# A two-layer decoder trunk: shorter filler at four waits, operands taken in smaller pieces, the S5 output product reordered, one sum of squares and one weight split moved

## The reference, cut to what matters

```
h = x
hn = rmsnorm(h);  h += retention(hn)        # 4 heads, q/k/v/g projections, per-head norm, output product
hn = rmsnorm(h);  h += swiglu(hn)           # dense, 1024 -> 3584 -> 1024
hn = rmsnorm(h);  h += s5(hn)               # u = hn @ w_in; complex diagonal scan over time;
                                            # y = Re(C state) + D u; gelu; z = y @ w_out; za * sigmoid(zb)
hn = rmsnorm(h);  h += moe(hn)              # logits = hn @ router; top 2 of 8 experts; each a swiglu
out = rmsnorm(h)
```

## Time and profile before

| | us |
|---|---|
| median of 3 runs | 1593.15 (1592.84 to 1593.97) |
| the profiled execution | 1591.9 |
| its span | 1589.7 |
| PE busy in the span | 1569.7 |
| DVE busy | 1212.1 |
| ACT busy | 984.6 |
| POOL busy | 264.4 |

### The profile page before, as it was taken

How to read it: one execution, slowest core, us unless ns; L and a number is a source line. 1 busy time by engine, 2 the same in 40 slices (tenths; PEclk the granted TensorE clock), 3 DMA queues, 4 the chain that set the end, 5 groups by cost and what they waited for, 6 DMA issues and landing times.

```text
span 1589.7 us, 23667 instructions
## 1 busy us (share of the span) xinstructions
PE 1569.7 (99%) x9522; PEld 1310.1 (82%) x9522; DVE 1212.1 (76%) x811; ACT 984.6 (62%) x731; POOL 264.4 (17%) x244
## 2 busy tenths in 40 slices
PE   8999999999999999999999999999999999999997
PEld 7888889999988778888888888888888888888886
DVE  5556566655557758888888888888888888888897
ACT  6444445333454356777777777777777777777775
POOL 5599215300036107100000000000000000000100
PEclk9999999999999999999999999999999999999999
DMA  9544648865511286999999999999999999999993
GB/s 350 165 157 158 211 139 283 281 201 186 186 54 56 78 309 242 395 385 363 386 354 366 395 366 352 388 360 368 382 379 347 389 376 344 393 372 349 399 393 150
DMA packets 202144, 469.19 MB, mean 295 GB/s; under 512 B 7785, under 2 KB 20289, under 8 KB 202065
## 3 DMA queue, kind: packets, MB, share of 16 engines
q1 hardware_dynamic: 199872, 461.13, 80.0%
q0 software_dynamic: 2048, 6.88, 1.5%
q10 hardware_dynamic: 144, 0.07, 0.0%
HBM read 461.23 MB, written 15.21 MB: 300 GB/s over the span
## 4 chain that ended last, share of the span: by engine, by line
PE 66%; DVE 1%; ACT 1%; issue 1%; POOL 0%; ACTq 0%; POOLq 0%; DVEq 0%
PE PS L1713 63%; PE PS L1832 2%; PE PS L2171 0%; ACT c_padded L878 0%; ACT weights_hi L878 0%; PE PS L2014 0%; POOL states L798 0%; DVE scan L1254 0%; DVE states L1254 0%; DVE weights_lo L1254 0%; PE PS L2129 0%; DVE scan_tmp L1254 0%; DVE residual L1254 0%; DVE normed_rows L1706 0%; DVE scan L1480 0%
## 5 line engine op out<-in xcount | busy, mean ns | idle before, releaser
L1254 DVE TENSOR_TENSOR weights_lo<-weights_raw,weights_hi 128x2048 fp32r<-128x2048 f32 (+1 forms) x419 | 964.3, 2310 | 263.7 <-ACT weights_hi L878 261.8
L878 ACT ACTIVATE weights_hi<-weights_raw 128x2048 fp32r<-128x2048 f32 (+1 forms) x419 | 800.7, 1912 | 366.4 <-PE PS L1713 354.0
L1713 PE MATMUL PS<-weights_hi,gathered_hi 128*128 128x512 f32 x896 | 355.3, 397 | 0.3 <-DVE gathered_lo L1594 0.3
L1713 PE MATMUL PS<-weights_hi,gathered_lo 128*128 128x512 f32 x896 | 355.0, 396 | 0.0
L1713 PE MATMUL PS<-weights_lo,gathered_hi 128*128 128x512 f32 x896 | 352.3, 393 | 0.0
L1713 PE MATMUL PS<-weights_hi,act_transposed_hi 128*128 128x512 f32 x624 | 252.9, 405 | 0.5 <-DVE act_transposed_lo L1402 0.5
L1713 PE MATMUL PS<-weights_hi,act_transposed_lo 128*128 128x512 f32 x624 | 247.0, 396 | 0.0
L1713 PE MATMUL PS<-weights_lo,act_transposed_hi 128*128 128x512 f32 x624 | 245.7, 394 | 0.0
L1713 PEld LDWEIGHTS PS<-weights_hi,gathered_lo 128*128 128x128 f32 x896 | 168.2, 188 | 41.3
L1713 PEld LDWEIGHTS PS<-weights_lo,gathered_hi 128*128 128x128 f32 x896 | 168.2, 188 | 41.1
L1713 PEld LDWEIGHTS PS<-weights_hi,gathered_hi 128*128 128x128 f32 x896 | 168.2, 188 | 39.9 <-DVE gathered_lo L1594 0.3
(11 more groups left out here) (279 smaller groups left out, 1273.6 us busy)
## 6 DMA issues: line engine op xcount, KB each, us to landing
weights_raw<-in_moe_w_up SPq DMA_DIRECT2D x111, 1024.0 KB, 7.3
weights_raw<-in_moe_w_down SPq DMA_DIRECT2D x111, 1024.0 KB, 7.0
weights_raw<-in_moe_w_gate SPq DMA_DIRECT2D x110, 1024.0 KB, 7.3
weights_raw<-in_ret_w_in SPq DMA_DIRECT2D x24, 1024.0 KB, 6.7
weights_raw<-in_ffn_w_gate SPq DMA_DIRECT2D x14, 1024.0 KB, 5.1
weights_raw<-in_ffn_w_up SPq DMA_DIRECT2D x14, 1024.0 KB, 5.1
weights_raw<-in_ffn_w_down SPq DMA_DIRECT2D x14, 1024.0 KB, 5.0
weights_raw<-in_ret_w_out SPq DMA_DIRECT2D x8, 1024.0 KB, 4.9
```

The lines of the kernel that those rows point to most:

```text
L878: return nc.scalar.activation(o, i, ACT.Copy)
L1254: return nc.vector.tensor_tensor(o, a, b, op)
L1713: return nc.tensor.matmul(o, l, r, start=start, stop=stop)
```

## The change

It does seven things:

1. `x_ready` asks for one pair instead of two before the first matmul, for the first (retention) and third (S5) norm; for the dense stage it still asks for two.
2. `yt_lo` is counted twice per head, behind tiles 0 and 1 and behind tiles 2 and 3; each half of the output product waits for its own half. The wait for `yt_hi` and the three fillers behind it go.
3. 16 fillers ahead of the dense stage become 9.
4. The six fillers in quarter 0 of S5 become three.
5. `s5_out` runs the direct products of both tiles first, with no wait for states, then all with the real states, then all with the imaginary ones, each behind its own wait.
6. The sum of squares of token tile 1 ahead of the routing goes from ACT (L1157) to DVE, and the low part of the second expert unit goes from ahead of the gate product to behind `pick`.
7. Five fillers between the two tiles of the logits become two.

```diff
@@ scalar, routing
             copy(hn_t[:, 0, :, :], PS[:, 0:2, :].rearrange("p a (b c) -> p (a b) c", c=P)).then_inc(hnt_copied[0], 1)
-            act.wait_ge(resid_ready, 3)
-            nc.scalar.activation(hn[:, 1, :], resid[:, 1, :], ACT.Square, accum_out=ssq[:, 1:2]).then_inc(ssq1_done, 1)
             act.wait_ge(ssq0_done, 4)
             act.wait_ge(ssq1_done, 4)
@@ vector, evac_yt
-                ins.then_inc(yt_lo, 1)
+                    if ft % 2:
+                        ins.then_inc(yt_lo, 1)
@@ vector, end of S5 and routing
-            for i in range(2):
-                split_lo(MOE_U0 + i)
+            split_lo(MOE_U0)
             dve.wait_ge(glu_read, 1)
             dve.wait_ge(glu_sig, 2)
...
+            dve.wait_ge(resid_ready, 3)
+            nc.vector.scalar_tensor_tensor(out=hn[:, 1, :], in0=resid[:, 1, :], scalar=1.0, in1=resid[:, 1, :],
+                                           op0=ALU.mult, op1=ALU.mult, accum_out=ssq[:, 1:2]).then_inc(ssq1_done, 1)
             dve.wait_ge(hnt_done, 2)
...
             ins.then_inc(pick_ready, 1)
 
+            split_lo(MOE_U0 + 1)
             dve.wait_ge(moe_landed, 32)
@@ tensor, x_ready
-                    pe.wait_ge(xlo_ready, KT // 2 * i + max(2, kt // 2 + 1))
+                    pe.wait_ge(xlo_ready, KT // 2 * i + max(2 if i == 1 else 1, kt // 2 + 1))
@@ tensor, retention
             def head_out(h, half, n):
+                pe.wait_ge(yt_lo, 2 * h + half + 1)
                 if half == 0:
-                    pe.wait_ge(yt_lo, h + 1)
                     pe.wait_ge(par_ready, 1)
...
             turn_y(HEADS - 1)
             idle_work(10, 0)
-            pe.wait_ge(yt_hi, HEADS)
-            idle_work(3, 0)
             head_out(HEADS - 1, 0, RET_UNITS - 2)
+            pe.wait_ge(yt_lo, 2 * HEADS)
             closing_unit(RET_UNITS - 1, ht_hi[0], ht_lo[0])
             plain(1)
-            idle_work(16, 4)
+            idle_work(9, 4)
             dense()
@@ tensor, s5_out
-                pe.wait_ge(st_re_ready, q + 1)
-                if q == QUARTERS - 1:
-                    pe.wait_ge(last_im_ready, 1)
-                else:
-                    pe.wait_ge(st_im_ready, q + 1)
                 y = PS[:, 5, :].rearrange("p (a c l) -> p a l c", a=QKT, l=STEP)
...
-                    for l in range(STEP):
-                        for j in range(2):
+                for j in range(2):
+                    if j == 0:
+                        pe.wait_ge(st_re_ready, q + 1)
+                    elif q == QUARTERS - 1:
+                        pe.wait_ge(last_im_ready, 1)
+                    else:
+                        pe.wait_ge(st_im_ready, q + 1)
+                    for a in range(QKT):
+                        for l in range(STEP):
                             for s in range(4):
@@ tensor, quarter 0
-                    idle_work(6, 5)
+                    idle_work(3, 5)
@@ tensor, logits
-                    idle_work(5, 4)
+                    idle_work(2, 4)
```

More of the change, by code:

```diff
@@ L1969, in _ @@
                 if h:
-                    pe.wait_ge(yt_lo, h)
+                    pe.wait_ge(yt_lo, 2 * h)
                 for half in range(2):
```

## The result

The changed kernel takes 1582.97 us (median of 6 runs, 1582.56 to 1583.54) against 1592.76 (1591.63 to 1593.97): 9.8 us less, ratio 0.994 with a 95% interval of 0.9929 to 0.995. 1587.3 had been forecast, in a range of 1585.0 to 1590.4, on a kernel before of 1593.15 (three runs; 1592.76 is the median of six). The profiled executions took 1582.77 us (span 1580.8) and 1591.9 (span 1589.7), 9.1 apart.

What follows compares the result with a forecast made beforehand. PE was taken as the bound, busy 1569.7 of 1589.7 us. Seven terms summed to 5.83, say 5.9 us, taken from 1593.15 to give 1587.3, in a range of 1585.0 to 1590.4.

Steps and rivals of the forecast that it cites:

- The fourth unit's low part: Kernel start: this work, ready at 31.16, does not move and lets PE in at 31.27, limiting the gain to 0.62.
- End of retention: Last head's output product: PE starts behind the second DVE instruction, at 207.76 instead of 208.54, gaining 0.78 us.
- Dense: Ahead of the dense stage: nine fillers instead of 16 gain 1.12 us, with DVE's two pairs then the limit.
- S5's first unit: One pair starts PE about 0.55 earlier, but the norm's diagonal does not move, so 0.35 us is gained.
- Quarter 0's filler: S5, six fillers to three: 0.7 us saved, but PE then idles 0.65 for POOL's padded B; gain 0.05.
- Routing and logits: Transposes 1.2 us earlier, logits 0.66, moved split 0.1 late behind `pick`: gain 1.76 us.
- The clock rival: Clock falls to 1.2 GHz behind the four filler cuts, costing 1.7 us each, up to 1594.2; chance 0.07.
- The rule weighed there: Routing: GpSimd shares SBUF interfaces with VectorE, so POOL's row numbers come some 2 us later beside the split; sum stays.
- s5_out, direct products first: S5 output products: same number of matmuls, waits of 0.2 (quarter 0) and 0.95 (last quarter) go; gain 1.15 us.
- The clock dip goes away: Rival, S5 near 496.70 to 500.15: the half clock also vanishes, 1.1 us more, 7.0 in all, 1586.1; chance 0.15.
- another hole of 0.65 us appears nearby: Argument against the clock dip going away: a new PE hole at 485.3.
- The start, 0.62: First unit, one pair instead of two: PE starts 0.78 us earlier, of which 0.62 lasts past the fourth unit.

Runs made afterwards that it cites:

- s5_out_only: Kernel before with only the new s5_out (direct products first, then each states part behind its own wait): 1589.58 us, ratio 0.9985.
- s5_order_only: Kernel before with s5_out's matmuls in the new order, but both waits for the states still ahead of all of them: 1591.9 us, ratio 0.9997.
- after_old_out: Changed kernel with only S5's output product as it was, both waits ahead and direct and state matmuls in turn: 1585.52 us, ratio 0.9952.
- before_again: Kernel before, unchanged, profiled a second time: 1592.53 us, ratio 1.0003.
- pairs_only: Kernel before with only the low parts of x asked for pair by pair, one pair ahead instead of two at first use: 1591.35 us, ratio 0.9996.
- before_start_fewer: Kernel before with ten filler matmuls fewer in its first 7 us, nothing else changed: 1591.18 us, ratio 0.9993.
- six_fillers: Changed kernel with six fillers ahead of s5_in(0) as before, instead of three: 1584.04 us, ratio 0.9947.
- fillers_but_q0: Kernel before with the filler cuts ahead of the dense layer, in the last head and in the router, but quarter 0's six kept: 1588.85 us, ratio 0.9976.
- q0_three_only: Kernel before with only the six fillers ahead of s5_in(0) cut to three: 1591.31 us, ratio 0.9992.
- six_fillers_load_late: Changed kernel with six fillers ahead of s5_in(0) and the 1 MB load issued only after the first quarter's output product: 1583.04 us, ratio 0.9939.
- late_load_split_behind: Changed kernel with the third S5 unit's low part behind quarter 0's states and the 1 MB load after that quarter's output product: 1583.93 us, ratio 0.9945.
- loads_late: Kernel before with a 1 MB weight load and POOL's 0.5 MB gain row load waiting for S5 output products, PE instructions unchanged: 1590.46 us, ratio 0.9989.
- after_start_more: Changed kernel with ten narrow matmuls (32 columns) more in its first 7 us: 1587.95 us (1585.49 to 1591.71), ratio 0.9973.
- split_behind_states: Changed kernel with the third S5 unit's low part moved on DVE from ahead of quarter 0's states to behind them: 1582.99 us, ratio 0.9941.

## Why the prediction was wrong

**What held.** The fourth unit's low part does bound the start; it came 0.5 later in this execution (29.09 for 28.58), and let PE on at 31.72 where 31.27 was said (31.89 before). End of retention: 0.78 said, 0.79 seen, with 0.34 idle. Dense: 1.12 and 1.14, bounded by DVE's second pair as said. S5's first unit: 0.35 and 0.3. Quarter 0's filler: nothing, and the new wait on POOL's b_padded of 0.69 where 0.65 was said. Routing and logits: 1.76 said; 1.2 + 0.70 - 0.05 = 1.85 seen. The experts kept everything. The clock rival did not come: 1.00 behind all four cuts. The rule weighed there came as said too: POOL's first routing instruction took 2.15 beside the moved split, where it had taken 1.14, and PE lost nothing by it.

**What failed.** *"s5_out, direct products first"*: the step reads "The number of matmuls is the same: 48 and 128", and took equal numbers for equal time, with 0.45 of room for a loss and 0.15 for a gain. The term was 1.15 and measures 0.22 + 0.95 + 4 x 0.25 = 2.17. Its two waits went as said; the regrouping gives 1.0 more, since it saves eight changes of tile form. That is shown in quarters 1 to 3 of s5_out_only and s5_order_only and in all four of after_old_out. The traces show it first: 32*32 products and 128*32 products in turn cost 0.12 to 0.14 us a change. The Trainium skill (TensorEngine Tiling (Array Packing), section "Tiling Modes", key properties) has the rule that I did not weigh: changing the tiling mode, not just the tile, drains TensorE. These runs agree with it; the page gives no price.

**The rival I gave 0.15 came half true.** "The clock dip goes away" was right on the size in quarter 0 (1.1) and wrong on the object. Without a half clock (before_again, pairs_only) s5_out(0) takes the same 6.16. What decides is where PE's instructions stand in the stream (before_start_fewer). That this acts through the supply of instructions is argued from the packets; only the pair of six_fillers shows it by itself. Of 18 profiled executions, eight show a stop of 0.24 to 0.54 in the small products near 493.7, and behind it three have the half clock and the five others a second stop of 0.21 to 1.29 in s5_out(0). Ten have no listed stop there and none of them the half clock, though four of the ten stop once later (pairs_only 0.91, six_fillers 1.21, and the two with late splits 0.70 and 0.45). The argument against it, "another hole of 0.65 us appears nearby", had nothing to do with it: padded B's wait does not make or heal the stop (fillers_but_q0, q0_three_only). With s5_in(0) (0.52), s5_out(0) (1.14) and the stop at 551.75 (0.5) this is 2.16 us that no term held: the sum gave nothing to a stretch for having its instructions moved in the stream. I had read PE's waits by what they wait for and passed over those marked "issue".

**What was not seen.** The start, 0.62: in this profile 0.05 is left, because the transposes of the normed rows came at 11.34 and not at 10.44, and so the pairs did. pairs_only, where they came at 10.01, shows 0.55. after_old_out, whose start is the changed kernel's, has them at 10.21, so this time varies between executions. The line of the kernel before:
```profile
10.44 1.91 PE L1802 MATMUL PS<-constants,normed_rows 128*128 128x128 f32 x16
```

Together: 5.83 - 0.57 (start) + 1.02 (order) + 2.16 (stops and quarter 0) + 0.25 (231 to 249, unexplained) + 0.12 (s5_in(1), unexplained) + 0.09 (routing and logits) = 8.9, of 9.0 at the experts and 9.1 between the profiled executions. From there to 9.8 the difference lies in the medians: the kernel before is profiled 0.9 below its median, the changed one 0.2. Of the 4.3 us between 1587.3 and 1582.97, 0.4 lie in the kernel before, which came out at 1592.76 and not 1593.15. The low end of the range was also added wrongly: the upper bounds and the dip gone are 7.5 + 1.1, so 1584.55 and not 1585.0; the measured time lies under both.

**Open.** Why a shift of ten fillers in the stream makes the difference, and in which direction, is not settled. That it does is shown by one profiled execution of a kernel with that edit alone (before_start_fewer) and by fillers_but_q0; where a packet must begin to do harm is not. Nor is why the half clock follows some stops and not others.

## What to carry to other kernels

Group small matmuls by tile form before counting them: a change of form (0.12 to 0.14 us) cost as much as two of the direct products (1.48 us for 24) or eight of the state products (1.03 for 64). Where PE runs hundreds of short instructions, read the stops marked "issue" and the instruction packets beside the weight loads, and if a 1 MB load lies there, try to make it wait for a later semaphore: it gave 1.0 us in six_fillers_load_late, and no gain in late_load_split_behind. And distrust small differences (one microsecond here) between two versions of such a kernel: they can come from where in the stream an instruction stands, which any edit moves; shift the stream by a harmless edit to tell.

## What the hardware showed

- A 1 MB load at 400 GB/s holds back PE's next 16 KB of instructions: 5.37 us from packet to packet with it (six_fillers), 3.46 without (six_fillers_load_late), and a stop of 1.21 us in PE for it.
- PE can stop in small products with no load near: in loads_late no weights are loaded from 487 to 503, packets start at 490.93 and 495.29, and PE stops 0.53 us up to 493.68.
- Ten filler matmuls fewer in the first 10 us change the time of a stretch at 497 us by 1.1 us, with PE arriving there within 0.13 us of before.
- Ten matmuls of 32 columns (20 records) took 2.25 us near the start of after_start_more, 0.11 per record, no less than the 128-column fillers (0.109 by the earlier trace rows).
- POOL's instructions for padded B depend on what DVE does beside them: the 128x256 form took 2.93 us beside the split of a weight unit in the changed kernel and 0.92 in split_behind_states, where the split comes later; the 128x768 form beside it there took 4.12 in place of 2.21. The Trainium skill (GPSIMD Engine Reference, table of specifications) has the two engines share their SBUF interfaces, and these rows agree.
